# Two transformer blocks on one core: grouped products in the transitions, late weight splits, norm roots read from PSUM

## The chip, the cores and the metric

One core of a Trainium2 chip runs the whole program. The metric is device time in microseconds (us) from launch to end, lower is better. The engines are TensorE (PE in the profile, with its weight loads as PEld), VectorE (DVE), ScalarE (ACT), GpSimd (POOL) and SyncE (SP), which issues all DMAs here. Every engine has a queue of its own that runs in order; the engines meet only at semaphores.

## The reference, cut to what matters

The input is 512 tokens of width 1024, in float32. A first block (neighbourhood attention and gated linear attention, merge, SwiGLU feed-forward) is followed by two layers of a second block (latent attention, convolution and retention side by side, merge, feed-forward). What the change touches is the frame of these blocks:

```
h = rms_norm(x, ln_mix_pre[l])
proj = h @ w_in[l]                      # first products: wide()
...
x = x + rms_norm(merged @ w_out[l], ln_mix_post[l])
h = rms_norm(x, ln_ffn_pre[l])
f = (silu(h @ ffn_w_gate[l]) * (h @ ffn_w_up[l])) @ ffn_w_down[l]
x = x + rms_norm(f, ln_ffn_post[l])
```

with `rms_norm(x, g) = x * rsqrt(mean(x*x) + 1e-6) * g`. A place where one norm ends and the next products begin is called a transition below.

## The kernel before, in words

Activations lie transposed: 128 features on the partitions, 512 tokens in the free dimension, eight such pages for a width of 1024. Every float32 product is made of three fast ones. An input page x is split into a first part (`hi`, x rounded to fp32r) and a remainder (`lo` = x - hi), and so is every weight tile. A product step `mm` (L1628) issues three matmuls of 128x512 into one PSUM bank: whi with hi (L1640), whi with lo (L1641), wlo with hi (L1642). It waits first for both parts of the input.

Weights arrive as 429 blocks of eight tiles. `w_load` (a DMA by SP) brings a block into one of three raw buffers; `w_split` rounds it on ACT (L1972) into one of four whi buffers and subtracts on POOL (L2913) into wlo. Block b may be split only when block b-4 is used up (semaphore `wdone`). The splits are placed in the program by `w_ahead` as the tiles are named, one at every fourth tile at most.

A plan written out by hand (`planned`, class `Plan`) makes one list of steps; each engine walks through the list and runs the functions that bear a step's name. The order of the list is so the order of each engine's queue.

Four products with the same inputs are made together by `wide` (L211): for each of the eight input pages k, four `mm` steps, one for each of four weight columns in four banks. It is called six times: for the first four columns of the first block's `w_out`; for the start of the first block's feed-forward; and for the start of the mixer and of the feed-forward in each of the two layers. Its argument `feed` is a generator that makes the input pages (three steps ahead, then one for each k). In the layers it is `post_norm`, which on DVE adds the scaled page to x (L2845, L2849), and `Input.hi`, which makes `in_hi` on ACT (L2199), its square on ACT (L2202), the `in_lo` of the page before on DVE (L2640) and the running sum of squares on DVE (L2652). The mixer of the first layer is the exception: its pages are made during the feed-forward before it, and it has no feed. The inputs aren't divided by their root mean square ahead of the products, but the results are: so in the four wides of the layers the argument `late` holds two steps. `late[0]` (`Input.root`) sums the squares over partitions (`square_rows`, L1716, on PE) and takes the root (`root`: L2325 on DVE, L1994 on ACT, L2325 again). `late[1]` spreads the root over a PSUM bank (`spread`, L1729, PE: it waits for the last DVE step of the root, L2340). Before, `late[0]` stands after the last product of k = 6 and `late[1]` after the last of k = 7.

A norm after a product (`post_norm`, and `norm_x2` in the first block) has the same steps without products between them: `rstd_rows` issues `square_rows`, the `root`, one filler matmul (`keep_warm`, L1740, which appears as two instructions), the `spread`, and three fillers. In these four the squares come as two pages (a sum and a tail); in the late ones as one. `root` on DVE first copies the sums from the bank (L2330 and an addition L2332 for two pages, L2334 for one), ACT takes logarithm (L1998) and exponential (L2000), and three small DVE steps refine it by one Newton step (L2336, L2338, L2340).

Of the kernel before, what the change touches and what calls it, by code (L numbers as in the profile page):

```python
# [11 lines left out]
ALU = mybir.AluOpType  # L12
# [8 lines left out]
NR, NH = 3, 4  # L21
# [135 lines left out]
class Plan:  # L157
# [53 lines left out]
    def wide(self, items, xs, late=None, feed=(), homes=None):  # L211

        feed = iter(feed)
        for _ in range(3):
            next(feed, None)
        outs = [(homes[i] if homes else self.mb).take(("o", *item)) for i, item in enumerate(items)]
        for k in range(8):
            next(feed, None)
            for (name, m), o in zip(items, outs):
                s = self.w_next((name, m, k))  # L220
                self.step("mm", s, ((o, xs[k]),), k == 0, k == 7)
                if late is not None and k == 6 and o is outs[-1]:
                    late[0]()
                if late is not None and k == 7 and o is outs[-1]:
                    late[1]()
                yield

    def turned(self, items, xs, outs, k0=0, held=0, done=None):
# [62 lines left out]
class Squares:  # L291
# [40 lines left out]
    def rows(self, n, bks):  # L332

        p, t = self.p, self.tag
        bks.take(("qm", t))
        p.row_of[t] = len(p.row_of)
        p.step("square_rows", t, self.n, self.tail)
        for i in (0, self.tail):
            if i is not None:
                p.pages.give(("q", t, i), ("qm", t))  # L340
        p.step("root", t, n, self.tail is not None)

    def rstd_rows(self, n, bks):

# [1059 lines left out]
def program(nc, a, out, p):  # L1404
    with ExitStack() as ctx:
        def sb(name, shape, dt=F32):
            return ctx.enter_context(nc.sbuf_tensor(name, shape, dt))

        def sem(name):
            return ctx.enter_context(nc.semaphore(name))  # L1410
# [9 lines left out]
        whi = sb("whi", [128, NH, 8, 128], F32R)  # L1420
        wlo = sb("wlo", [128, NH, 8, 128], F32R)
# [17 lines left out]
        lin, dot, turn = (Signal(sem(n), at) for n in ("s_linear", "s_dot", "s_turn"))  # L1439
        whid, acp, fun = (Signal(sem(n), at) for n in ("s_whi", "s_copied", "s_function"))  # L1440
        vec = Signal(sem("s_vector"), at)
# [6 lines left out]
        def when(*name):  # L1448
            return at.get(name, (None, 0)) if counting[0] else at[name]
# [6 lines left out]
        ident, ones, bones = cst[:, 0, :], cst[:, 1, :], cst[:, 2, :]  # L1456
# [6 lines left out]
        def col(name, i=0, n=1):  # L1463
            o = PCOL[name][0] + i
            return prm[:, o:o + n]

        def F(name):
            return pageF[p.pages.place[name]][:, :]

        def R(name):  # L1470
            return pageR[p.pages.place[name]][:, :]

        def bank(name):
            return banks[p.mb.place[name] if name in p.mb.place else 4 + p.sbk.place[name]][:, :]
# [4 lines left out]
        def over(name):  # L1479

            for homes in (p.pages, p.mb, p.sbk):
                if name in homes.over:
                    return homes.over[name]

        def half(x, part):

            if x[0] == "HC":
                return R(x)[:, 0:256] if part == "hi" else R(x)[:, 256:512]
            return R((*x, part))
# [19 lines left out]
        def rows(t, i):  # L1509

            o = 256 + 12 * p.row_of[t] + 4 * i
            return smal[:, o:o + 4]
# [108 lines left out]
        def tensor(e):  # L1621
            w = Hand(e)

            def clear(name):
                for k in over(name):
                    w.wait_ge(*when(*k))

            def mm(s, groups, first, last):  # L1628
# [4 lines left out]
                for n, (name, x) in enumerate(groups):  # L1633
# [12 lines left out]
                    if names:  # L1646
                        i.then_inc(*lin.up(*names))

            def mm_turned(s, n, outs, x, first, last, final):
                a, ring = s % (8 * NH), 8 * NH  # L1650
                hi, lo = (y[:, :, :, :].rearrange("p b j f -> p (b j) f") for y in (whi, wlo))
                for b in range(s // 8, (s + n - 1) // 8 + 1):
                    w.wait_ge(*when("whi", b))
                    w.wait_ge(*when("wlo", b))
                w.wait_ge(*when(*x, "hi"))
                w.wait_ge(*when(*x, "lo"))
                for t, name in outs:
                    if first:
                        clear(name)
                    xh, xl = (half(x, part)[:, 128 * t:128 * t + 128] for part in ("hi", "lo"))  # L1660
                    for c, d in ((0, min(n, ring - a)), (ring - a, n)):
                        if c < d:
                            o, at0 = bank(name)[:, 128 * c:128 * d], (a + c) % ring
                            h, r = hi[:, at0:at0 + d - c, :], lo[:, at0:at0 + d - c, :]
                            e.matmul(o, xh, h, start=first and c == 0, stop=False, skip_group_check=True)  # L1665
                            e.matmul(o, xl, h, start=False, stop=False, skip_group_check=True)  # L1666
                            i = e.matmul(o, xh, r, start=False, stop=last and d == n, skip_group_check=True)  # L1667
                    names = [name] if last else []
                    if final and t == outs[-1][0]:
                        names += [("wdone", b) for b in range(s // 8, (s + n) // 8)]  # L1670
                    if names:
                        i.then_inc(*lin.up(*names))
# [43 lines left out]
            def square_rows(t, n, tail):  # L1716
                o = bank(("qm", t))
                clear(("qm", t))
                w.wait_ge(*when("cst"))
                w.wait_ge(*(when("q", t, 0) if n == 1 else when("qa", t, n - 1)))  # L1720
                for c, i in ((0, 0), (4, tail)):
                    if i is not None:
                        w.wait_ge(*when("q", t, i))
                        for j in range(4):
                            x = e.matmul(o[:, c + j:c + j + 1], F(("q", t, i))[:, 128 * j:128 * j + 128], ones[:, 0:1],
                                         start=True, stop=True)
                x.then_inc(*dot.up(("qm", t)))

            def spread(t):  # L1729
# [207 lines left out]
            def ret_values(l, h, i):  # L1937
# [6 lines left out]
                t.then_inc(*dot.up(("ro", l, h, i)))  # L1944

            mine = {f.__name__: f for f in (
                mm, mm_turned, mod_mm, first_sums, square_rows, spread, keep_warm, mod_columns, square_sum, to_tokens, x_turned, mod_sum,
                gla_gate, gla_gate_ctx, gla_state0, gla_states, gla_scores, gla_out, na_scores, na_values, mla_scores, mla_values, soft_rows, conv_mean, ret_scores,
                ret_values)}
            for kind, *what in p.steps:  # L1950
# [4 lines left out]
        def scalar(e):  # L1955
            w = Hand(e)
# [23 lines left out]
            def log_exp():  # L1980
                if loaded[0] != "both":
                    loaded[0] = "both"
                    e.preload_act_table_set("natural_log_exp_and_others")
# [7 lines left out]
                w.wait_ge(*fun.last())  # L1991
                e.activation(r, r, ACT.Exp, scale=-0.5).then_inc(*fun.up(("re", t)))

            def root(t, n, two):  # L1994
                x, r = rows(t, 2), rows(t, 0)
                log_exp()
                w.wait_ge(*when("qs", t))
                e.activation(r, x, ACT.Ln, scale=1.0 / n, bias=col("eps")).then_inc(*fun.up())  # L1998
                w.wait_ge(*fun.last())
                e.activation(r, r, ACT.Exp, scale=-0.5).then_inc(*fun.up(("re", t)))  # L2000
# [290 lines left out]
        def vector(e):  # L2291
            w = Hand(e)

            def clear(name):
                for k in over(name):
                    w.wait_ge(*when(*k))

            def after():
                w.wait_ge(*vec.last())
# [22 lines left out]
                after()  # L2322
                e.scalar_tensor_tensor(r, x, 1.5, r, ALU.add, ALU.mult).then_inc(*vec.up(("rr", t)))

            def root(t, n, two):  # L2325
                o = bank(("qm", t))
                r, s, x = (rows(t, i) for i in range(3))
                w.wait_ge(*when("qm", t))
                if two:
                    e.tensor_copy(s, o[:, 0:4]).then_inc(*vec.up())  # L2330
                    after()
                    e.tensor_tensor(x, s, o[:, 4:8], ALU.add).then_inc(*vec.up(("qs", t)))  # L2332
                else:
                    e.tensor_copy(x, o[:, 0:4]).then_inc(*vec.up(("qs", t)))  # L2334
                w.wait_ge(*when("re", t))
                e.scalar_tensor_tensor(s, r, -0.5 / n, r, ALU.mult, ALU.mult).then_inc(*vec.up())  # L2336
                after()
                e.scalar_tensor_tensor(s, x, n * EPS, s, ALU.add, ALU.mult).then_inc(*vec.up())  # L2338
                after()
                e.scalar_tensor_tensor(r, s, 1.5, r, ALU.add, ALU.mult).then_inc(*vec.up(("rcol", t)))  # L2340
# [600 lines left out]
        for engine in (sync, tensor, scalar, vector, gpsimd):  # L2941
            engine(Dry())
# [4 lines left out]
        block = ctx.enter_context(nc.Block())  # L2947
        block.sync(sync)
        block.tensor(tensor)
        block.scalar(scalar)  # L2950
        block.vector(vector)
# [181 lines left out]
```

## Time and profile before

| what | value |
|---|---|
| median of 3 runs | 2908.97 us (2908.12 to 2909.49) |
| profiled execution, its own time | 2907.14 us |
| its span, first to last instruction | 2905.3 us |
| PE busy | 2827.4 us, 97% |
| DVE, ACT, POOL busy | 1290.8, 1131.3, 1186.1 us |
| split on ACT, mean of 429 | 1053 ns |
| split on POOL, mean of 429 | 2427 ns |

A row of the timeline gives the start in the span, the duration, the engine, the line, what is written and read, how many like it were merged into the row, and in brackets how long the engine had been idle and who ended that. A matmul's duration contains its latency: in a dense stretch the starts are much closer than the durations.

### The profile page before, as it was taken

The page shows a single profiled execution, that of the slowest core. Times are in us where ns is not written, and L with a number is a line of the kernel's source. Part 1 is how long each engine was busy: PE and PEld are TensorE (multiplying, and loading weights), DVE is VectorE, ACT ScalarE, POOL GpSimd, SP SyncE. Part 2 cuts the span into 40 slices and gives each one's busy share as a digit, 9 for nine tenths or more (in the row PEclk, how much of TensorE's full clock was granted, in tenths as well). Part 3 has the DMA queues.
Part 4 walks back from the last instruction along what each step waited for, and adds up shares of the span by engine and source line. Part 5 has one row for each costly group of instructions (what it writes and reads, how often), then busy time and mean ns, then how long its engine had stood idle before and what let it go on. Part 6 is the DMA issues. An engine that isn't in the chain of part 4 may idle for free.

```text
span 2905.3 us, 34409 instructions
## 1 busy us (share of the span) xinstructions
PE 2827.4 (97%) x13708; PEld 2242.9 (77%) x13708; DVE 1290.8 (44%) x1714; ACT 1131.3 (39%) x1681; POOL 1186.1 (41%) x539
## 2 busy tenths in 40 slices
PE   7999999999999999999999999999999999999999
PEld 6787678788888776787787888867767868788887
DVE  4776424511113866835315202277677353341123
ACT  4334643432233555433334222245545233432222
POOL 2123233344443662453443444435624434344443
PEclk9999999999999999999999999999999999999999
DMA  7343223333333211232232323332102323233232
GB/s 255 116 152 126 76 83 99 110 113 96 96 100 125 80 59 37 72 94 73 88 123 77 98 94 102 95 104 79 66 30 73 102 66 110 93 98 99 94 95 80
DMA packets 89278, 277.97 MB, mean 96 GB/s; under 512 B 9952, under 2 KB 10272, under 8 KB 89120
## 3 DMA queue, kind: packets, MB, share of 16 engines
q1 hardware_dynamic: 89120, 275.78, 29.4%
q8 instruction: 109, 1.79, 0.3%
q14 instruction: 49, 0.40, 0.0%
HBM read 268.40 MB, written 7.34 MB: 95 GB/s over the span
## 4 chain that ended last, share of the span: by engine, by line
PE 87%; DVE 9%; ACT 3%; issue 1%; SPq 0%; DMA 0%; DVEq 0%; ACTq 0%
PE bank L1640 24%; PE bank L1642 24%; PE bank L1641 24%; PE bank L1750 2%; PE bank L1943 2%; PE bank L1893 2%; PE bank L1665 1%; PE bank L1666 1%; PE bank L1667 1%; PE bank L1905 1%; PE bank L1934 1%; DVE pageR L2640 1%; DVE pageF L2775 1%; PE bank L1710 1%; PE bank L1880 1%
## 5 line engine op out<-in xcount | busy, mean ns | idle before, releaser
L2913 POOL TENSOR_TENSOR wlo<-wraw,whi 128x1024 fp32r<-128x1024 f32 x429 | 1039.9, 2427 | 1489.5 <-ACT whi L1972 1482.1
L1640 PE MATMUL bank<-pageR,whi 128*128 128x512 f32 (+1 forms) x3376 | 1366.7, 405 | 20.0 <-DVE pageR L2640 8.2
L1642 PE MATMUL bank<-pageR,wlo 128*128 128x512 f32 (+1 forms) x3376 | 1306.4, 387 | 0.0
L1641 PE MATMUL bank<-pageR,whi 128*128 128x512 f32 (+1 forms) x3376 | 1305.5, 387 | 0.0
L1640 PEld LDWEIGHTS bank<-pageR,whi 128*128 128x128 f32 x3376 | 636.0, 188 | 186.7 <-issue 60.3
L1641 PEld LDWEIGHTS bank<-pageR,whi 128*128 128x128 f32 x3376 | 636.8, 189 | 143.6 <-issue 24.0
L1642 PEld LDWEIGHTS bank<-pageR,wlo 128*128 128x128 f32 x3376 | 635.4, 188 | 131.6
L1972 ACT ACTIVATE whi<-wraw 128x1024 fp32r<-128x1024 f32 x429 | 450.5, 1053 | 408.7 <-PE bank L1642 343.3
L2056 ACT ACTIVATE pageR<-pageF 128x512 fp32r<-128x512 f32 x136 | 86.0, 632 | 444.8 <-DVE pageF L2634 196.1
L2775 DVE SCALAR_TENSOR_TENSOR pageF<-pageF,prm 128x497 f32<-128x497 f32 (+9 forms) x180 | 200.0, 1111 | 2.7
L2629 DVE TENSOR_TENSOR pageF<-bank,pageF 128x512 f32<-128x512 f32 x44 | 30.4, 690 | 212.9 <-PE bank L1642 209.0
L2922 POOL TENSOR_TENSOR pageR<-pageF,pageR 128x512 fp32r<-128x512 f32 x46 | 66.0, 1450 | 137.3 <-ACT pageR L2056 129.7
L2086 ACT ACTIVATE pageF<-bank 128x512 f32<-128x512 f32 (+1 forms) x148 | 82.8, 575 | 96.4 <-PE bank L1750 95.9
L2157 ACT ACTIVATE pageF<-bank,smal 128x512 f32<-128x512 f32 x96 | 65.9, 686 | 135.2 <-DVE smal L2540 135.1
L2632 DVE TENSOR_TENSOR pageF<-pageF,bank 128x512 f32<-128x512 f32 x44 | 30.2, 687 | 197.0 <-PE bank L1642 163.7
L2933 POOL TENSOR_TENSOR pageF<-pageF 128x497 f32<-128x497 f32 (+14 forms) x60 | 82.2, 1370 | 67.9 <-ACT pageF L2252 67.3
L1750 PEld LDWEIGHTS bank<-cst,pageF 128*128 128x128 f32 x564 | 67.9, 141 | 45.2 <-ACT pageF L2157 15.8
L1750 PE MATMUL bank<-cst,pageF 128*128 128x128 f32 x564 | 85.0, 277 | 15.8 <-ACT pageF L2061 8.6
L2402 DVE TENSOR_TENSOR pageR<-pageF,pageR 128x512 fp32r<-128x512 f32 x90 | 67.1, 745 | 64.7 <-ACT pageR L2056 64.7
L2591 DVE SCALAR_TENSOR_TENSOR pageF<-pageF,bank 128x512 f32<-128x512 f32 x64 | 43.9, 685 | 110.2 <-PE bank L1642 109.9
L2226 ACT ACTIVATE pageF<-pageF 128x512 f32<-128x512 f32 x56 | 35.3, 631 | 140.6 <-DVE pageF L2695 140.6
L2312 DVE TENSOR_TENSOR pageF<-pageF 128x512 f32<-128x512 f32 x40 | 38.5, 963 | 115.3 <-ACT pageF L1978 114.9
(239 smaller groups left out, 2305.6 us busy)
## 6 DMA issues: line engine op xcount, KB each, us to landing
wraw<-in_wst SPq DMA_DIRECT2D x429, 512.0 KB, 3.5
pageF<-in_wmod SPq DMA_DIRECT2D x96, 256.0 KB, 4.5
pageF<-in_xT SPq DMA_DIRECT2D x16, 256.0 KB, 4.4
pageF<-in_bias SPq DMA_DIRECT2D x16, 256.0 KB, 3.9
kept<-pageF SPq DMA_DIRECT2D x16, 256.0 KB, 4.5
pageF<-kept SPq DMA_DIRECT2D x16, 256.0 KB, 4.0
out_x<-pageF SPq DMA_DIRECT2D x8, 256.0 KB, 2.0
pageF<-in_cT SPq DMA_DIRECT2D x4, 256.0 KB, 6.4
```

Source lines behind the costliest of these rows:

```text
L1640: e.matmul(o, hi, xh, start=first, stop=False)
L1641: e.matmul(o, hi, xl, start=False, stop=False)
L1642: i = e.matmul(o, lo, xh, start=False, stop=last)
L1750: t = e.transpose(o[:, 128 * j:128 * j + 128], x[:, c:c + 128], ident)
L1972: e.activation(whi[:, b % NH, :, :], wraw[:, b % NR, :, :], ACT.Copy).then_inc(*whid.up(("whi", b)))
L2056: e.activation(R((*x, "hi")), F(src), ACT.Copy).then_inc(*acp.up((*x, "hi")))
L2086: e.activation(F(dst)[:, 0:n], bank(("tb", dst))[:, 0:n], ACT.Copy).then_inc(*acp.up(dst))
L2402: e.tensor_tensor(R((*x, "lo")), F(src), bc(R((*x, "hi"))), ALU.subtract).then_inc(*vec.up((*x, "lo")))
L2775: e.scalar_tensor_tensor(acc, x, c, acc, ALU.mult, ALU.add).then_inc(*vec.up(("tapd", l, m, n)))
L2913: e.tensor_tensor(wlo[:, b % NH, :, :], wraw[:, b % NR, :, :], bc(whi[:, b % NH, :, :]), ALU.subtract).then_inc(*wlod.up(("wlo", b)))
L2922: e.tensor_tensor(R((*x, "lo")), F(src), bc(R((*x, "hi"))), ALU.subtract).then_inc(*low.up((*x, "lo")))
L2933: e.tensor_tensor(acc, acc, F(("tap", l, n))[:, 0:hi - lo], ALU.add).then_inc(*low.up(("tapd", l, m, n)))
```

## The change

In `wide`, the four products of one k are no longer four `mm` steps but two: `mm_first_part` waits for the `hi` of the page and issues whi·hi and wlo·hi for all four columns, `mm_second_part` waits for the `lo` and issues whi·lo for all four. `late[0]` now stands between the two parts of k = 7, `late[1]` behind the second. The splits that `w_ahead` would place at k = 1 to 4 are left to k = 5, 6 and 7. In `square_rows` both pages of squares are summed in the bank, and `root` reads this bank itself, on ACT and in the middle DVE step; the copy and the addition on DVE are gone.

```diff
         for k in range(8):
             next(feed, None)
-            for (name, m), o in zip(items, outs):
-                s = self.w_next((name, m, k))
-                self.step("mm", s, ((o, xs[k]),), k == 0, k == 7)
-                if late is not None and k == 6 and o is outs[-1]:
-                    late[0]()
-                if late is not None and k == 7 and o is outs[-1]:
-                    late[1]()
+            slots = [self.w_slot((name, m, k)) for name, m in items]
+            if k == 0 or k > 4:
+                self.w_ahead(*slots)
+            self.step("mm_first_part", tuple(slots), tuple(outs), xs[k], k == 0)
+            if late is not None and k == 7:
+                late[0]()
+            self.step("mm_second_part", tuple(slots), tuple(outs), xs[k], k == 7)
+            if late is not None and k == 7:
+                late[1]()
+            for _ in items:
                 yield
...
+            def mm_first_part(slots, outs, x, first):
+                xh = half(x, "hi")
+                w.wait_ge(*when(*x, "hi"))
+                for s, name in zip(slots, outs):
...
+                    e.matmul(bank(name), whi[:, b % NH, j, :], xh, start=first, stop=False)
+                    e.matmul(bank(name), wlo[:, b % NH, j, :], xh, start=False, stop=False)
+
+            def mm_second_part(slots, outs, x, last):
+                xl = half(x, "lo")
+                w.wait_ge(*when(*x, "lo"))
+                for s, name in zip(slots, outs):
...
+                    i = e.matmul(bank(name), whi[:, b % NH, j, :], xl, start=False, stop=last)
...
+                pages_in = (0,) if tail is None else (0, tail)
+                for i in pages_in:
+                    w.wait_ge(*when("q", t, i))
+                    for j in range(4):
+                        x = e.matmul(o[:, j:j + 1], F(("q", t, i))[:, 128 * j:128 * j + 128], ones[:, 0:1],
+                                     start=i == 0 and j == 0, stop=i == pages_in[-1] and j == 3, skip_group_check=True)
...
             # root on ACT
-                x, r = rows(t, 2), rows(t, 0)
+                x, r = bank(("qm", t))[:, 0:4], rows(t, 0)
-                w.wait_ge(*when("qs", t))
+                w.wait_ge(*when("qm", t))
...
             # root on DVE
-                o = bank(("qm", t))
-                r, s, x = (rows(t, i) for i in range(3))
+                x, r, s = bank(("qm", t))[:, 0:4], rows(t, 0), rows(t, 1)
                 w.wait_ge(*when("qm", t))
-                if two:
-                    e.tensor_copy(s, o[:, 0:4]).then_inc(*vec.up())
-                    after()
-                    e.tensor_tensor(x, s, o[:, 4:8], ALU.add).then_inc(*vec.up(("qs", t)))
-                else:
-                    e.tensor_copy(x, o[:, 0:4]).then_inc(*vec.up(("qs", t)))
```

## Rows read from the trace of the kernel before

**Rows 1.** The page's busy times: engine, us, share, instructions.
```profile
PE 2827.4 (97%) x13708; PEld 2242.9 (77%) x13708; DVE 1290.8 (44%) x1714; ACT 1131.3 (39%) x1681; POOL 1186.1 (41%) x539
```

**Rows 2.** Timeline, root of the norm ahead of layer 0's feed-forward.
```profile
1523.17 0.16 DVE L2330 COPY smal<-bank 128x4 f32<-128x4 f32 x1 [5.86 <-PE bank L1725]
...
1523.56 0.30 ACT L1998 ACTIVATE smal<-smal,prm 128x4 f32<-128x4 f32 x1 [1.04 <-DVE smal L2332]
...
1524.74 0.38 PE L1733 MATMUL bank<-cst,smal 128*128 128x128 f32 x1 [0.63 <-DVE smal L2340]
```

**Rows 3.** Timeline, layer 0's feed-forward wide: the feed and PE's waits.
```profile
1529.71 0.47 PE L1640 MATMUL bank<-pageR,whi 128*128 128x512 f32 x1 [1.24 <-ACT pageR L2199]
...
1535.99 2.50 POOL L2913 TENSOR_TENSOR wlo<-wraw,whi 128x1024 fp32r<-128x1024 f32 x1 [15.41 <-ACT whi L1972]
...
1536.16 2.88 DVE L2640 SCALAR_TENSOR_TENSOR pageR<-pageF,prm,pageR 128x512 fp32r<-128x512 f32 x1
...
1539.19 0.47 PE L1640 MATMUL bank<-pageR,whi 128*128 128x512 f32 x1 [1.07 <-DVE pageR L2640]
...
1546.60 0.47 PE L1640 MATMUL bank<-pageR,whi 128*128 128x512 f32 x1 [1.69 <-DVE pageR L2640]
```

**Rows 4.** Line L2640, all 32 of it: ns min/median/max.
```profile
L2640 DVE SCALAR_TENSOR_TENSOR pageR<-pageF,prm,pageR x32: 739/744/2885, 861.9 to 2549.4; 128x512 fp32r<-128x512 f32 x32
```

**Rows 5.** Timeline, the end of the same wide.
```profile
1548.47 0.73 ACT L2199 ACTIVATE pageR<-pageF,prm 128x512 fp32r<-128x512 f32 x1 [3.53 <-DVE pageF L2849]
...
1549.62 1.99 ACT L1972 ACTIVATE whi<-wraw 128x1024 fp32r<-128x1024 f32 x2
...
1550.83 4.74 POOL L2913 TENSOR_TENSOR wlo<-wraw,whi 128x1024 fp32r<-128x1024 f32 x2 [4.93 <-ACT whi L1972]
...
1552.16 0.95 PE L1725 MATMUL bank<-cst,pageF 128*128 128x1 f32 x8
...
1553.90 1.69 DVE L2336 SCALAR_TENSOR_TENSOR smal<-smal 128x4 f32<-128x4 f32 x1 [0.60 <-ACT smal L2000]
...
1556.04 1.16 PE L1733 MATMUL bank<-cst,smal 128*128 128x128 f32 x8
```

**Rows 6.** Timeline near 952 us: DVE and POOL, instructions behind each other.
```profile
951.73 1.37 DVE L2772 TENSOR_SCALAR pageF<-pageF,prm 128x512 f32<-128x512 f32 x1
...
952.78 5.36 POOL L2913 TENSOR_TENSOR wlo<-wraw,whi 128x1024 fp32r<-128x1024 f32 x2
...
953.14 2.75 DVE L2775 SCALAR_TENSOR_TENSOR pageF<-pageF,prm 128x497 f32<-128x497 f32 x1
```

**Rows 7.** Line L2629, which reads one bank and one page: ns min/median/max.
```profile
L2629 DVE TENSOR_TENSOR pageF<-bank,pageF x44: 681/691/693, 1557.9 to 2832.9; 128x512 f32<-128x512 f32 x44
```

**Rows 8.** Timeline, the end of layer 0's mixer wide.
```profile
925.94 0.16 DVE L2334 COPY smal<-bank 128x4 f32<-128x4 f32 x1 [16.56 <-PE bank L1725]
...
928.62 1.05 PE L1733 MATMUL bank<-cst,smal 128*128 128x128 f32 x8
```

**Rows 9.** Windows: busy us (count) of each engine, granted clock (PEclk), DMA share, GB/s.
```profile
83.42:90.23 6.81, 5.98 (x20) 5.27 (x21) 5.70 (x11) 3.71 (x10) 0.00 (x0) 0.50 0.00 0
540.80:544.20 3.40, 3.40 (x11) 1.97 (x10) 0.68 (x5) 0.50 (x2) 0.00 (x0) 0.50 0.00 0
1230.30:1233.70 3.40, 1.27 (x6) 0.62 (x4) 3.00 (x5) 3.32 (x4) 1.20 (x1) 1.00 0.00 0
1233.70:1237.10 3.40, 3.40 (x9) 2.31 (x8) 1.16 (x2) 2.53 (x3) 1.44 (x1) 0.50 0.25 31
```

**Rows 10.** Timeline, matmuls at the lower granted clock.
```profile
1235.56 0.63 PE L1640 MATMUL bank<-pageR,whi 128*128 128x512 f32 x1
1235.99 0.63 PE L1641 MATMUL bank<-pageR,whi 128*128 128x512 f32 x1
```

**Rows 11.** Timeline, PE's waits in layer 1's mixer and feed-forward wide.
```profile
1939.66 0.67 PE L1710 MATMUL bank<-pageF,cst 128*128 128x512 f32 x1 [0.93 <-DVE pageF L2312]
...
2546.37 0.47 PE L1640 MATMUL bank<-pageR,whi 128*128 128x512 f32 x1 [1.68 <-DVE pageR L2640]
```

More of the change, by code:

```diff
@@ L340, in rows @@
                 p.pages.give(("q", t, i), ("qm", t))
-        p.step("root", t, n, self.tail is not None)
+        p.step("root", t, n)
     def rstd_rows(self, n, bks):
@@ L1647, in mm @@
                         i.then_inc(*lin.up(*names))
+            def mm_first_part(slots, outs, x, first):
+                xh = half(x, "hi")
+                w.wait_ge(*when(*x, "hi"))
+                for s, name in zip(slots, outs):
+                    b, j = divmod(s, 8)
+                    w.wait_ge(*when("whi", b))
+                    w.wait_ge(*when("wlo", b))
+                    if first:
+                        clear(name)
+                    e.matmul(bank(name), whi[:, b % NH, j, :], xh, start=first, stop=False)
[4 more added lines that the diff above has]
+                for s, name in zip(slots, outs):
+                    b, j = divmod(s, 8)
+                    i = e.matmul(bank(name), whi[:, b % NH, j, :], xl, start=False, stop=last)
+                    names = [name] if last else []
+                    if j == 7:
+                        names.append(("wdone", b))
+                    if names:
+                        i.then_inc(*lin.up(*names))
             def mm_turned(s, n, outs, x, first, last, final):
@@ L1720, in square_rows @@
                 w.wait_ge(*(when("q", t, 0) if n == 1 else when("qa", t, n - 1)))
[L1721 to L1726, printed above, removed]
+                pages_in = (0,) if tail is None else (0, tail)
[4 more added lines that the diff above has]
+                                     start=i == 0 and j == 0, stop=i == pages_in[-1] and j == 3, skip_group_check=True)
                 x.then_inc(*dot.up(("qm", t)))
@@ L1946, in tensor @@
             mine = {f.__name__: f for f in (
-                mm, mm_turned, mod_mm, first_sums, square_rows, spread, keep_warm, mod_columns, square_sum, to_tokens, x_turned, mod_sum,
+                mm, mm_first_part, mm_second_part, mm_turned, mod_mm, first_sums, square_rows, spread, keep_warm, mod_columns, square_sum, to_tokens, x_turned, mod_sum,
                 gla_gate, gla_gate_ctx, gla_state0, gla_states, gla_scores, gla_out, na_scores, na_values, mla_scores, mla_values, soft_rows, conv_mean, ret_scores,
@@ L1992, in rstd_act, with root @@
                 e.activation(r, r, ACT.Exp, scale=-0.5).then_inc(*fun.up(("re", t)))
-            def root(t, n, two):
-                x, r = rows(t, 2), rows(t, 0)
+            def root(t, n):
+                x, r = bank(("qm", t))[:, 0:4], rows(t, 0)
                 log_exp()
-                w.wait_ge(*when("qs", t))
+                w.wait_ge(*when("qm", t))
                 e.activation(r, x, ACT.Ln, scale=1.0 / n, bias=col("eps")).then_inc(*fun.up())
@@ L2323, in rstd_dve, with root @@
                 e.scalar_tensor_tensor(r, x, 1.5, r, ALU.add, ALU.mult).then_inc(*vec.up(("rr", t)))
-            def root(t, n, two):
-                o = bank(("qm", t))
-                r, s, x = (rows(t, i) for i in range(3))
+            def root(t, n):
+                x, r, s = bank(("qm", t))[:, 0:4], rows(t, 0), rows(t, 1)
                 w.wait_ge(*when("qm", t))
-                if two:
-                    e.tensor_copy(s, o[:, 0:4]).then_inc(*vec.up())
-                    after()
-                    e.tensor_tensor(x, s, o[:, 4:8], ALU.add).then_inc(*vec.up(("qs", t)))
-                else:
-                    e.tensor_copy(x, o[:, 0:4]).then_inc(*vec.up(("qs", t)))
                 w.wait_ge(*when("re", t))
```

## The prediction

> **What bounds the kernel now.** I read the busy times first. PE is busy 97% of the span [rows 1], so time can only be won where PE waits, or lost where it comes to wait. Next I went through PE's rows in order of time for the brackets that show a wait, and looked up the regions that the change touches, with all engines side by side. Seven places matter: four norms after a product, in which nothing but fillers covers the root; three wides with a feed (layer 0's feed-forward, both of layer 1's); and the late steps of all four layer wides (the fourth is layer 0's mixer, whose pages are ready).
>
> In a norm, from the copy of the sums to the spread are 1.57 us, and PE idles 0.63 us before the spread [rows 2].
>
> In a wide with a feed PE waits three times, 1.24, 1.07 and 1.69 us [rows 3]; the other two have the same waits, the last of them 1.68 us in layer 1's feed-forward [rows 11]. The first is the first page's remainder. The others have a cause that lies on POOL. At 1535.99 the split's subtraction starts; at 1536.16 DVE starts `in_lo`, and it takes 2.88 us instead of the line's median of 0.74 [rows 3, 4]. It ends 0.5 us after POOL's. So DVE stood still while POOL subtracted. A step that reads a bank and a page shows nothing of the kind in 44 cases, 681 to 693 ns [rows 7]. The root has it too: its first DVE step, of four columns, takes 1.69 us from 1553.90, and ends where POOL's second subtraction ends, 1550.83 + 4.74 = 1555.57 [rows 5]. When POOL has one subtraction behind another, a blocked DVE step gets in between: the one started at 951.73 ends at 953.10, next to POOL's start at 952.78, and the next one, from 953.14, is held again to 955.89 [rows 6]. This is the point on which my forecast rests.
>
> **The root read from the bank.** Two DVE steps go where there are two pages: 1523.56 - 1523.17 = 0.39 us; for one page I take half, 0.20 [rows 2]. The middle DVE step now reads a bank and one small page, so POOL can't hold it [rows 7]; the first and the third still read two operands in SBUF. That the read from a bank costs ACT or DVE more is not seen: L2629 with a bank is at 0.69 us [rows 7]; bounds -0.1 to +0.1 us a step, I take 0. In the norm ahead of the first feed-forward the 0.39 us are PE's own waiting. The clock is at 1.2 GHz there (0.50 granted from 540.80 to 544.20 [rows 9]) and fillers follow that run slower if they come earlier, so I count -0.3 (0 to -0.39). The other three norms stand in front of wides, below. The number of matmuls is unchanged, so summing in the bank costs nothing.
>
> **First parts ahead, in layer 0's feed-forward.** The start: PE needs only the first page's `hi`, so the 1.24 us go and PE starts about 1.6 us earlier with the norm's 0.39. Of this little is left at k = 3: the split of k = 0 stays where it was, behind the fourth `in_hi` on ACT, and still holds `in_lo` of that page. This one is released at 1539.19 - 0.39 = 1538.80. What moves is that only four matmuls of k = 3 wait for it instead of twelve. The split of k = 2, which made the 1.69 us, goes behind the feed, and DVE's feed is 2.88 - 0.74 = 2.14 us earlier from there on: 2.53 with the norm. A matmul takes (1552.16 - 1546.60)/24 = 0.23 us [rows 3, 5]. The feed makes a page in less than twelve of them, so nothing more waits, and from 1538.80 PE has 4 + 36 + 8 = 48 matmuls to `square_rows`: 1538.80 + 11.04 = 1549.84, where before it was 1552.16. So 2.3 us are won up to this point.
>
> **The end of that wide.** In the old order twelve products (2.8 us) covered the root, now it is four (0.9 us). From `square_rows` to the root's first DVE step it was 1553.90 - 1552.16 = 1.74 us, less the copy 1.54: 1551.38. PE ends its second part at 1549.84 + 0.95 + 0.92 = 1551.7.
> But the deferred splits are now all here. ACT has three, not two, right behind the last `in_hi` and square: from 1549.62 - 2.53 = 1547.1, done by 1550.1, so ACT's part of the root isn't late. POOL's three start at 1550.83 - 2.53 = 1548.30 and take 4.74/2 = 2.37 us each [rows 5]: they end at 1550.67, 1553.04 and 1555.41. The root's first DVE step (1551.38) meets the second subtraction and gets in at 1553.04. The middle one is free. The third comes 0.2 us later, meets the third subtraction, and ends with it at 1555.4. The spread follows at 1555.5, against 1556.04 before. Of the 2.3 us just 0.54 are left, and PE idles 3.8 us in one piece where it idled 4 us in three. The spread releases all that follows, so this is the gain of the whole wide. The splits themselves come no later: the last one ends at 1555.4 where the last ended at 1555.57, and the loads behind them on SP's queue wait for nothing new. If this cover were gone, each us of delay would be one of the span, as PE is dense behind.
>
> **The other wides.** Layer 1's two have the same waits and the same order: -0.54 each. In layer 0's mixer wide nothing waits for pages. There the order costs: ACT's part of the root starts eight matmuls after the old copy, 925.94 + 1.84 = 927.78, the spread comes 1.57 - 0.39 = 1.18 us later, at 928.96, against 928.62 [rows 8]: +0.34. ACT is idle there, so the splits go as soon as blocks are free and don't move. The first block's two wides have no wait and no late step: 0.
>
> **The clock.** An idle piece of 3.8 us is new in this part of the kernel. At 1233.06 a wait of PE ended, in a stretch with 1.27 us busy of 3.40; the granted clock then was 0.50 for 3.4 us [rows 9]: 2.4 GHz became 1.2. A matmul takes 0.43 us in it [rows 10]. In the old feed-forward wides no stretch at 0.50 shows. I expect one in each of the three: behind the idle piece it costs 3.4 x (1 - 0.23/0.43) = 1.6 us if all of it falls on dense work, nothing if it falls into the wait. I take 1.1, nearer to what happened at 1233.7. In layer 1's mixer PE waits 0.93 us for DVE soon after [rows 11] and that swallows most: 0.2.
> The Trainium skill, TensorE: Matmul & The Clock Gate, "What's actually happening", says that the throttled clock is the default state and that activity releases it. By it the sum below keeps its 2.4 us for the clock; were only the average share of work to count, those would be dropped and the kernel would come out 1.6 us faster.
>
> **The sum.** -0.3 (norm) + 0.34 (layer 0's mixer) - 3 x 0.54 (wides) + 1.1 + 1.1 + 0.2 (clock) = +0.8 us. The profiled execution took 2907.14 us (2905.3 and 1.8 around it) and lies 1.8 us under the median; the difference carries over: 2908.97 + 0.8 = 2909.8 us.
>
> **Rivals.**
> *One subtraction is escaped* (0.14). If `square_rows` came 0.7 us earlier, the root's first step would meet the first subtraction (to 1550.67) and the third step the second, to 1553.04. Spread at 1553.1, 2.9 us gained in each, no long idle: -8.7, so 2900.3 us. For: the margin is only 0.7 us in a chain of 11 us. Against: both ends hang on the same DVE feed.
> *The root runs free* (0.12). If the small steps slip in, or the split of k = 0 no longer meets `in_lo` (it started just 0.17 us ahead, 1535.99 against 1536.16 [rows 3]), the spread comes 1.54 + 0.61 us after `square_rows`, about 1552.0: -4.05 each, -12.2 in all, 2896.8 us. Against: the 1.69 us of [rows 5].
> *The clock stays low* (0.09), the case on the slow side. From 83.42 to 90.23 it was 0.50 for 6.8 us [rows 9]. If the fall comes inside the idle piece at the spread and a second such stretch joins on, about 5 to 6.8 us of dense work run at 0.43 us: 2.4 to 3.2 us each, less 0.9 in layer 1's mixer. +6.3 to +8.7 - 1.6: 2914 to 2916 us. [...] Against: in [rows 9] one wait of some 2 us brought one short stretch.
> *The change doesn't do what it says* (0.03): another wait holds k = 3 or the first part, and all stays within 1 us.
>
> **How the numbers follow.** The forecast has 0.62. What this kernel's measurement can tell from no change is 0.2%, 5.8 us: below 2903.2 or above 2914.8. Faster are the first two rivals and little else: 0.27. Slower is most of the third, 0.09. The rest, 0.64, is the same. The range takes in the first rival and most of the third and leaves out the second: 2899 to 2915 us. The forecast's own range is 2907 to 2913.
>
> **What would show it.** Three POOL subtractions back to back just after the last `in_hi` of a wide; L2336 and L2340 both long there (up to 2.4 us) and L2338 short; PE waiting some 3.8 us before the spread for L2340; one `in_lo` at 2.9 us in each wide, not two; no wait at k = 0 and about 0.7 us ahead of the second part of k = 3; 0.3 us ahead of the spread in layer 0's mixer; a granted clock of 0.50 after three of the spreads. If L2340 stays at 0.16 us everywhere, the forecast is wrong and a rival holds.

## The result, and the profile after

| | before | changed |
|---|---|---|
| median of 17 runs | 2910.32 us | 2914.87 us |
| profiled execution's span | 2905.3 us | 2912.3 us |
| PE busy | 2827.4 us | 2834.4 us |

The ratio is 1.0018 (1.0011 to 1.0024): the change costs 0.18%, some 5 us. It was forecast at +0.8 us. The spans of the two profiled executions differ by 7.0 us, the medians by 4.55: the profiled executions took 2907.14 and 2914.15 us, so they lie 3.2 and 0.7 us under their medians. PE did the same 13708 matmuls and was busy 7 us longer, which no wait explains; this points to the clock.

In the lines of the changed kernel the first DVE step of the root is L2356, the middle one L2358, the last L2360; the spread is L1760, `square_rows` L1752, the second part L1669, `in_lo` L2660, the split L1999 on ACT and L2933 on POOL. The norm ahead of layer 0's feed-forward, timeline of the changed kernel (it answers to [rows 2]):

```profile
1524.38 0.26 ACT L2025 ACTIVATE smal<-bank,prm 128x4 f32<-128x4 f32 x1 [0.65 <-PE bank L1752]
...
1524.98 0.16 DVE L2356 SCALAR_TENSOR_TENSOR smal<-smal 128x4 f32<-128x4 f32 x1 [6.46 <-ACT smal L2027]
1525.18 0.16 DVE L2358 SCALAR_TENSOR_TENSOR smal<-bank,smal 128x4 f32<-128x4 f32 x1
1525.37 0.16 DVE L2360 SCALAR_TENSOR_TENSOR smal<-smal 128x4 f32<-128x4 f32 x1
1525.59 0.60 PE L1760 MATMUL bank<-cst,smal 128*128 128x128 f32 x3 [0.28 <-DVE smal L2360]
```

ACT starts where the copy was, and reads the bank in 0.26 us instead of 0.30; the middle DVE step is 0.16 us as before. PE's wait is 0.28 us instead of 0.63. Then the wide behind it, first the middle (it answers to [rows 3]):

```profile
1536.85 2.50 POOL L2933 TENSOR_TENSOR wlo<-wraw,whi 128x1024 fp32r<-128x1024 f32 x1 [15.06 <-ACT whi L1999]
1537.01 2.89 DVE L2660 SCALAR_TENSOR_TENSOR pageR<-pageF,prm,pageR 128x512 fp32r<-128x512 f32 x1
...
1539.96 0.51 PE L1669 MATMUL bank<-pageR,whi 128*128 128x512 f32 x1 [0.47 <-DVE pageR L2660]
```

and its end (it answers to [rows 5]):

```profile
1548.36 2.94 ACT L1999 ACTIVATE whi<-wraw 128x1024 fp32r<-128x1024 f32 x3
...
1549.57 7.01 POOL L2933 TENSOR_TENSOR wlo<-wraw,whi 128x1024 fp32r<-128x1024 f32 x3 [10.22 <-ACT whi L1999]
...
1551.01 0.95 PE L1752 MATMUL bank<-cst,pageF 128*128 128x1 f32 x8
1551.82 1.19 PE L1669 MATMUL bank<-pageR,whi 128*128 128x512 f32 x4
...
1552.61 1.69 DVE L2356 SCALAR_TENSOR_TENSOR smal<-smal 128x4 f32<-128x4 f32 x1 [2.92 <-ACT smal L2027]
1554.33 0.16 DVE L2358 SCALAR_TENSOR_TENSOR smal<-bank,smal 128x4 f32<-128x4 f32 x1
1554.53 2.07 DVE L2360 SCALAR_TENSOR_TENSOR smal<-smal 128x4 f32<-128x4 f32 x1
```

All three subtractions are back to back. The root's first step is held to the end of the second. The middle one reads a bank and passes during the third. The last one is held to the end of the third. The spreads of the three wides with a feed, PE's timeline:

```profile
1556.65 1.65 PE L1760 MATMUL bank<-cst,smal 128*128 128x128 f32 x6 [3.64 <-DVE smal L2360]
...
1933.75 1.65 PE L1760 MATMUL bank<-cst,smal 128*128 128x128 f32 x6 [3.67 <-DVE smal L2360]
...
2560.02 1.22 PE L1760 MATMUL bank<-cst,smal 128*128 128x128 f32 x4 [3.66 <-DVE smal L2360]
```

and layer 0's mixer (it answers to [rows 8]):

```profile
929.64 1.16 PE L1760 MATMUL bank<-cst,smal 128*128 128x128 f32 x8 [0.21 <-DVE smal L2360]
```

What comes behind the long waits, windows of the changed kernel (it answers to [rows 9]; the granted clock is the number after POOL's):

```profile
1555.70:1562.50 6.80, 5.85 (x18) 4.99 (x19) 2.72 (x4) 2.51 (x3) 0.88 (x1) 0.50 0.37 142
1562.50:1570.00 7.50, 7.50 (x35) 6.18 (x34) 4.21 (x7) 4.32 (x6) 1.36 (x1) 1.00 0.00 0
1931.10:1937.90 6.80, 4.15 (x14) 3.67 (x15) 3.87 (x6) 2.04 (x4) 2.90 (x3) 0.50 0.74 246
2559.20:2566.00 6.80, 5.98 (x18) 5.11 (x19) 2.72 (x4) 2.51 (x3) 0.75 (x1) 0.50 0.37 146
```

The clock is at 1.2 GHz for 6.8 us, not 3.4. It falls inside the wait, 2.7 us after its start in layer 0's feed-forward (at 1555.7, where the spread starts at 1556.65), 1.0 us in the mixer (at 1931.1) and 2.8 us in layer 1's feed-forward (at 2559.2). Behind it, matmuls start 0.43 us apart:

```profile
1558.95 0.63 PE L1644 MATMUL bank<-pageR,whi 128*128 128x512 f32 x1
1559.38 0.63 PE L1645 MATMUL bank<-pageR,wlo 128*128 128x512 f32 x1
```

To place the time I take the distances between spreads, from the timelines of each kernel (us). The other kernels are described with the experiments below. Up to the norm where the first column starts, changed, old_late, both and ffn_behind are 0.3 to 0.9 us later than before and fill is 1.8; two_splits is 6.5 us later, 4.2 of them lost behind the spread of layer 0's mixer against the changed kernel.

| kernel | norm to spread, layer 0's feed-forward | to the next norm | norm to spread, layer 1's mixer | to the next norm | norm to spread, layer 1's feed-forward | to the end |
|---|---|---|---|---|---|---|
| before | 31.30 | 342.62 | 31.19 | 594.66 | 31.31 | 349.48 |
| changed | 31.06 | 345.38 | 31.72 | 595.22 | 31.05 | 352.28 |
| fill | 31.07 | 343.16 | 31.73 | 594.27 | 31.07 | 349.46 |
| two_splits | 27.63 | 342.27 | 27.50 | 598.53 | 27.63 | 349.50 |
| old_late | 29.68 | 342.30 | 29.59 | 595.96 | 28.78 | 349.54 |
| ffn_behind | 27.61 | 342.29 | 30.98 | 595.95 | 27.63 | 349.47 |
| both | 28.54 | 342.29 | 28.67 | 594.35 | 27.62 | 349.51 |

The two feed-forward wides won what was forecast, nearly nothing. The loss lies behind them: 2.76 and 2.80 us behind the feed-forward spreads, 0.6 us behind the mixer's (0.95 against fill). Some norms have a low stretch of the clock of their own, which makes a number 0.5 to 0.9 us larger: changed and fill in the second and third column, old_late in the first and third, both in the first. In old_late and ffn_behind a low stretch near 2232 us makes the fourth number 1.6 us larger. With such a stretch layer 1's mixer wide is 0.53 us longer in the changed kernel, and not shorter. The price of the first long wait is thus known less well than the 2.80 us of the last. Against fill the second column is 2.2 us longer, but fill's own stretch at that norm is 6.8 us and the changed kernel's is 3.4, so this is too little; against the kernels without a stretch there (342.3) it is 3.1 us, which is too much. The profile before has no low stretch at that norm; why the changed kernel and fill have one isn't known.

### The profile page after: what moved, and what is told of

Its sections match the earlier page's. It is cut to its first block, busy times and chain, and to the rows that moved or that the text cites. A ratio compares the mean times of both kernels' runs of the same rounds, so it can differ in the third digit from the quotient of the medians.

```text
span 2912.3 us, 34371 instructions
## 1 busy us (share of the span) xinstructions
PE 2834.4 (97%) x13708; PEld 2250.6 (77%) x13708; DVE 1294.3 (44%) x1702; ACT 1131.1 (39%) x1681; POOL 1184.6 (41%) x539
## 4 chain that ended last, share of the span: by engine, by line
PE 87%; DVE 9%; ACT 2%; issue 1%; SPq 0%; DMA 0%; DVEq 0%; ACTq 0%
PE bank L1643 23%; PE bank L1645 23%; PE bank L1644 23%; PE bank L1970 2%; PE bank L1777 2%; PE bank L1920 2%; PE bank L1692 1%; PE bank L1693 1%; PE bank L1694 1%; PE bank L1662 1%; PE bank L1661 1%; PE bank L1669 1%; PE bank L1932 1%; PE bank L1961 1%; DVE pageF L2595 1%
## 5 line engine op out<-in xcount | busy, mean ns | idle before, releaser
L2933 POOL TENSOR_TENSOR wlo<-wraw,whi 128x1024 fp32r<-128x1024 f32 x429 | 1038.5, 2423 | 1498.0 <-ACT whi L1999 1497.4
L1643 PE MATMUL bank<-pageR,whi 128*128 128x512 f32 x3184 | 1293.4, 406 | 8.1 <-DVE pageR L2398 3.2
L1645 PE MATMUL bank<-pageR,wlo 128*128 128x512 f32 x3184 | 1234.6, 388 | 0.0
L1644 PE MATMUL bank<-pageR,whi 128*128 128x512 f32 x3184 | 1233.3, 387 | 0.0
L1643 PEld LDWEIGHTS bank<-pageR,whi 128*128 128x128 f32 x3184 | 601.6, 189 | 162.1 <-issue 43.0
L1644 PEld LDWEIGHTS bank<-pageR,whi 128*128 128x128 f32 x3184 | 601.8, 189 | 136.5 <-issue 23.9
L1645 PEld LDWEIGHTS bank<-pageR,wlo 128*128 128x128 f32 x3184 | 600.3, 189 | 123.8
L1999 ACT ACTIVATE whi<-wraw 128x1024 fp32r<-128x1024 f32 x429 | 450.3, 1053 | 407.1 <-PE bank L1645 318.9
```

Source lines behind the costliest of these rows:

```text
L1643: e.matmul(o, hi, xh, start=first, stop=False)
L1644: e.matmul(o, hi, xl, start=False, stop=False)
L1645: i = e.matmul(o, lo, xh, start=False, stop=last)
L1999: e.activation(whi[:, b % NH, :, :], wraw[:, b % NR, :, :], ACT.Copy).then_inc(*whid.up(("whi", b)))
L2933: e.tensor_tensor(wlo[:, b % NH, :, :], wraw[:, b % NR, :, :], bc(whi[:, b % NH, :, :]), ALU.subtract).then_inc(*wlod.up(("wlo", b)))
```

## The experiments

My theory after the result: (1) POOL's subtractions set the time of the spread; (2) the long wait that they leave in one piece brings the clock down for 6.8 us, and this is the loss. The rival: the new order of the products, or its extra waits, costs by itself. All these kernels were timed beside the kernel before.

**fill.** The wait is filled.

```diff
+                fill()          # p.keep_warm(sbk, 3) in the three wides with a feed
                 late[1]()
```

> The changed kernel with three filler matmuls (six instructions, some 2.8 us) between the second part of k = 7 and the spread, in the three wides with a feed. Theory (trap and clock): POOL's three subtractions still hold the spread at the same time, but PE no longer idles 3.6 us, so no stretch at 0.50 follows the spread and the 2.8 us per feed-forward wide go: ratio to before 0.9995 (0.998 to 1.000). Rival (the new order of products and waits itself costs, the low clock is a bystander): ratio stays at 1.0018.

Measured: 0.9999 (0.9990 to 1.0008). PE waits 1.08 us instead of 3.64, the spread comes at the same distance (31.07 against 31.06 us), and the clock holds, in the windows around the spread:

```profile
1550.00:1557.00 7.00, 6.52 (x28) 4.20 (x26) 4.04 (x5) 2.72 (x5) 6.47 (x3) 1.00 0.34 87
1557.00:1564.00 7.00, 6.39 (x32) 5.47 (x33) 3.14 (x5) 3.15 (x4) 0.53 (x1) 1.00 0.39 140
```

So the loss is the clock's: work that computes nothing wins it back. The rival falls: fill has the new order and all other waits, and costs nothing against before.

**last_split** and **two_splits.** Splits go behind the spread.

```diff
-            if k == 0 or k > 4:
-                self.w_ahead(*slots)
+            if k == 0 or k > 4:
+                if late is not None and k in (6, 7):      # last_split: (7,)
+                    held.extend(slots)
+                else:
+                    self.w_ahead(*slots)
...
                 late[1]()
+                for s in held:
+                    self.w_ahead(s)
```

> The changed kernel, but where a wide has late steps only the split of k = 7 is placed behind the spread. Theory (trap): the first DVE step of the root is held by the second subtraction (about 1.7 us), the third step is free, the spread is 2.9 us earlier than before the change, PE idles 1.3 us, no low clock: ratio 0.997. Rival (the number of subtractions doesn't matter, only ACT's queue does): spread earlier by ACT's 1 us only, low clock stays, ratio 1.001.

Measured: 0.9989 (0.9980 to 0.9997). The mechanism is as expected, DVE's timeline of last_split:

```profile
1553.70 1.69 DVE L2361 SCALAR_TENSOR_TENSOR smal<-smal 128x4 f32<-128x4 f32 x1 [2.90 <-ACT smal L2032]
1555.43 0.16 DVE L2363 SCALAR_TENSOR_TENSOR smal<-bank,smal 128x4 f32<-128x4 f32 x1
1555.62 0.16 DVE L2365 SCALAR_TENSOR_TENSOR smal<-smal 128x4 f32<-128x4 f32 x1
```

One step is held instead of two. The size is a third of what I expected. A part goes in the mixers, where the deferred split holds another chain (below), and a part to the clock: PE waits 1.74 us, and behind that there still is a low stretch, here of 3.4 us:

```profile
1556.30:1559.70 3.40, 3.40 (x13) 2.92 (x12) 0.69 (x1) 2.11 (x3) 0.42 (x1) 0.50 0.56 161
```

> The changed kernel, but where a wide has late steps the splits of k = 6 and 7 are placed behind the spread; that of k = 5 stays. Theory (trap): the root's first DVE step comes 0.7 us after the only subtraction ahead of it, both long steps go back to 0.16 us, the spread comes about 4 us earlier than before the change in each of three wides, PE idles 0.3 us ahead of it, no low clock: ratio 0.9958 (0.995 to 0.997). Rival (splits placed late starve the weights, or the root is held by something else than POOL): PE waits for wlo behind the spread, ratio 1.000 or more.

Measured: 0.9981 (0.9973 to 0.9990). No root step is held, and norm to spread is 27.50 to 27.63 us: 3.7 less than before, 4.0 with the norm's 0.35, in all three wides. But less than half of these 12 us arrives. The rest, some 8 us, is lost in the mixers, where the deferred subtractions meet other DVE steps. POOL's and DVE's timelines of two_splits, layer 0's mixer, and PE's:

```profile
934.04 7.97 POOL L2938 TENSOR_TENSOR wlo<-wraw,whi 128x1024 fp32r<-128x1024 f32 x3 [16.65 <-ACT whi L2004]
```
```profile
937.00 2.77 DVE L2730 TENSOR_TENSOR pageF<-pageF 32x512 f32<-32x512 f32 x1
939.80 2.76 DVE L2732 TENSOR_TENSOR pageF<-pageF 32x512 f32<-32x512 f32 x1
```
```profile
945.09 1.10 PE L1742 MATMUL bank<-pageF,cst 128*128 128x512 f32 x2 [3.52 <-DVE pageF L2344]
```

PE waits 3.52 us there where it waited 0.92 in the changed kernel, and the stretch behind layer 1's mixer is 598.53 us instead of the 594.66 of before (here a low stretch of 3.4 us, behind another wait of 3.50 us, takes a part). In this kernel a subtraction has its price where DVE has a chain that PE waits for; behind a feed-forward spread it shows none (342.27 us to the next norm, as in old_late and both).

**early_splits.** The splits are where they were, products and root as changed.

```diff
-            if k == 0 or k > 4:
-                self.w_ahead(*slots)
+            self.w_ahead(*slots)
```

> The changed kernel with the splits at k = 2, 4 and 6 again, as before the change. Theory: the split of k = 2 holds one in_lo for 2.9 us again, the first parts hide part of it, square_rows comes 0.5 us earlier than before the change, one root step is held by the second of two subtractions, the spread is 0.4 us earlier than before and PE idles 2.0 us ahead of it, which may or may not bring a low stretch: ratio 0.9995 to 1.0005. Rival (grouping the products alone costs): ratio 1.0015 or more with the same clock as before.

Measured: 1.0001 (0.9992 to 1.0010). PE waits 1.65 us for a held `in_lo` again and 1.87 us ahead of the spread. Two of the three spreads are followed by a low stretch of 3.4 us. Grouping the products, with the new root, shows neither a cost nor a gain in the time as long as the splits aren't late; what the grouping alone would be worth without these low stretches no run shows.

**splits_only.** The kernel before with the late splits alone.

```diff
                 s = self.w_slot((name, m, k))        # was w_next
+                if k == 0 or k > 4:
+                    self.w_ahead(s)
```

> The kernel before with only the splits of k = 1 to 4 left to k = 5, 6 and 7. Theory: the wait of 1.69 us at k = 5 goes; square_rows comes 1.9 us earlier; the root, still with its copy, meets the second subtraction with its first step and the third with its second (its middle step reads SBUF here): spread at about the old time, PE idles some 2.2 us ahead of it, perhaps with a low stretch: ratio 1.0000 to 1.0010. Rival (late splits alone are the gain and the grouping is the loss): ratio 0.998 or less.

Measured: 1.0002 (0.9993 to 1.0011). Here the middle step of the root has both operands in SBUF, and it is the one that the third subtraction holds:

```profile
1554.81 1.54 DVE L2338 SCALAR_TENSOR_TENSOR smal<-smal 128x4 f32<-128x4 f32 x1 [0.60 <-ACT smal L2002]
1556.38 2.27 DVE L2340 SCALAR_TENSOR_TENSOR smal<-smal 128x4 f32<-128x4 f32 x1
1558.69 0.16 DVE L2342 SCALAR_TENSOR_TENSOR smal<-smal 128x4 f32<-128x4 f32 x1
```

Norm to spread is 31.30 us, as before to the hundredth: what the late splits win at the feed, the root gives back. The first and second step are held and the third is free, as forecast.

**root_only.** The root read from the bank, all else as before.

> The kernel before with the root read from the bank alone: products in single steps, splits and late steps in the old places. Theory: four norms are 0.39 us shorter, the root's middle step can't be held; the spreads come 0.4 us earlier: -1.5 us, ratio 0.9995 (0.999 to 1.000). Rival (reading the bank costs ACT or DVE some 0.1 to 0.2 us a step and the norms gain nothing): ratio 1.000 and the span from copy to spread unchanged at 1.57 us.

Measured: 1.0000 (0.9991 to 1.0008). The norm is shorter as expected, PE waits 0.28 us instead of 0.63 ahead of the spread. In the profiled execution layer 1's mixer spread comes 0.8 us earlier than before; a low stretch of the clock at 2233.8, which the profile of before hasn't, then takes this back. This measurement can't tell a gain of 1.5 us from none: the rows show shorter norms, the times show no gain.

**old_late.** The root goes back behind k = 6.

```diff
-            if late is not None and k == 7:
-                late[0]()
             self.step("mm_second_part", tuple(slots), tuple(outs), xs[k], k == 7)
+            if late is not None and k == 6:
+                late[0]()
```

> The changed kernel with late[0] (square_rows and root) back behind k = 6, splits late as changed. Theory: square_rows comes 1.3 us earlier than in the changed kernel, the root's first step meets the first subtraction and its third the second, and ACT does the third split only after the root: the spread is some 2.9 us earlier than before the change in three wides, twelve products stand ahead of it so PE idles about 1.4 us, no long low clock; in layer 0's mixer nothing is lost. Ratio 0.997. Rival (the place of the root is without effect, only the number of splits ahead counts as program order has it): the third step is held by the third subtraction all the same, ratio 1.000 or more.

Measured: 0.9973 (0.9964 to 0.9982), as forecast. DVE's and PE's timelines of old_late:

```profile
1552.05 0.50 DVE L2356 SCALAR_TENSOR_TENSOR smal<-smal 128x4 f32<-128x4 f32 x1 [1.77 <-ACT smal L2027]
1552.58 0.16 DVE L2358 SCALAR_TENSOR_TENSOR smal<-bank,smal 128x4 f32<-128x4 f32 x1
1552.78 2.10 DVE L2360 SCALAR_TENSOR_TENSOR smal<-smal 128x4 f32<-128x4 f32 x1
```
```profile
1554.93 1.16 PE L1760 MATMUL bank<-cst,smal 128*128 128x128 f32 x8 [0.68 <-DVE smal L2360]
```

Its first step comes 0.5 us ahead of the end of the first subtraction, in the changed kernel 0.7 us behind it. It is the same chain of steps and the same subtractions; which of them it meets differs, and that is 2.3 us in a wide (28.78 against 31.05). PE's wait is 0.7 us instead of 3.6. No low stretch follows the spreads of these wides.

**ffn_behind.** The two splits go behind the spread in the layers' feed-forward wides only (`behind=rs is not None`); layer 1's mixer has fillers.

> The changed kernel with the splits of k = 6 and 7 behind the spread in the two feed-forward wides of the layers only, three filler matmuls ahead of the spread in layer 1's mixer, and layer 0's mixer as changed. Theory: each feed-forward wide keeps its 4 us, and the 3.9 us that two_splits lost in each mixer (two DVE steps of the rope behind the spread held by subtractions, 2.8 us each) don't come back: some -8.7 us against before, ratio 0.997. Rival (what two_splits lost belongs to the low stretches of the clock, wherever they fall): ratio 0.998 to 0.999 again.

Measured: 0.9977 (0.9968 to 0.9986), between the two forecasts, so the ratio doesn't decide. The table does: each feed-forward wide keeps its 3.7 us, no wait of 3.5 us shows in the mixers, and the stretch behind layer 1's mixer is 2.6 us shorter than in two_splits although both kernels have one low stretch of 3.4 us in it. So at least this part of what two_splits lost belongs to the subtractions. The span is 2899.0 us, 6.3 below before's.

**both.** `late[0]` as in old_late in the mixers, splits as in ffn_behind in the feed-forwards.

> The two better forms put together: in the feed-forward wides of the layers the splits of k = 6 and 7 behind the spread and late[0] between the parts of k = 7; in the two mixer wides late[0] behind k = 6 and the splits late as changed. Theory (each wide's price is its own): two feed-forward wides give 4.1 us each, layer 1's mixer 1.6 to 2.5 us, the norm 0.3, layer 0's mixer nothing: -11 us, ratio 0.9962 (0.995 to 0.997). Rival (what is won at a spread is lost again behind it): 0.9973 as old_late.

Measured: 0.9963 (0.9949 to 0.9977), median 2898.13 us beside 2908.51 for before: the lowest median, 0.37% under the kernel before and some 0.55% under the changed one. Its interval overlaps with that of old_late, so it isn't shown to be faster than that one. In the two feed-forward wides the root runs free, and the clock is at 2.4 GHz behind the spread (in layer 1's mixer the root's last step is still held, 2.11 us):

```profile
1553.05 0.16 DVE L2363 SCALAR_TENSOR_TENSOR smal<-smal 128x4 f32<-128x4 f32 x1 [2.89 <-ACT smal L2034]
...
1553.44 0.16 DVE L2367 SCALAR_TENSOR_TENSOR smal<-smal 128x4 f32<-128x4 f32 x1
```
```profile
1553.66:1560.40 6.74, 6.74 (x34) 5.72 (x35) 1.73 (x3) 4.41 (x5) 3.83 (x2) 1.00 0.27 84
```

## Why the prediction was right and wrong

The waits came out as worked out, in number, place and size. The term that failed is the clock's, and it was the largest.

- *The norms*: PE's wait shrank by 0.35 us (0.39 forecast) ahead of layer 0's feed-forward. In the norm ahead of the first feed-forward, `square_rows` to spread went from 2.66 to 2.31 us (0.3 forecast; 2.51 in root_only). Reading the bank costs nothing more.
- *The feed*: one `in_lo` held, none at k = 0 waited for. PE waited 0.47 us at k = 3 (0.7 forecast).
- *The trap*: both long steps are there, 1.69 and 2.07 us, the middle one 0.16; PE's wait is 3.64 to 3.67 us (3.8 forecast). The spreads of the two feed-forwards came 0.24 to 0.26 us nearer to their norms, 0.6 with the norm's part (0.54 forecast); that of layer 1's mixer is 0.53 us farther, with a low stretch of the clock at its norm that the forecast hadn't. That a bank operand frees the middle step rested on [rows 7], which doesn't say whether POOL was at work: the trace of before has 33 of these 44 steps overlapping a subtraction, so the reading holds.
- *Layer 0's mixer*: 0.21 us of wait (0.3 forecast). But the time from the norm ahead of the first feed-forward to this spread grew from 386.38 to 387.02 us, by 0.64 (+0.34 forecast). With the root back behind k = 6 (old_late) it still is 386.71: the place of the root is about half of it, and what the other half is stays open.
- *The clock*: this is the step that failed. "I expect one in each of the three: behind the idle piece it costs 3.4 x (1 - 0.23/0.43) = 1.6 us if all of it falls on dense work, nothing if it falls into the wait. I take 1.1." The low stretch was 6.8 us and not 3.4, and some 5.9 us of it lay on work in each feed-forward: 2.2 to 3.1 us in layer 0's and 2.8 us in layer 1's, against 1.1. In the mixer PE's wait for DVE vanished in it, as forecast, and it still cost 0.6 to 0.95 us against 0.2. With 2.6 (an estimate, the middle of 2.2 and 3.1), 2.8 and 0.8 for the clock the sum is -0.3 + 0.3 - 1.8 + 2.6 + 2.8 + 0.8 = +4.4 us; the medians differ by 4.55. So close an agreement is partly luck: the sum holds neither the low stretch at layer 1's mixer norm nor the 0.3 us more of layer 0's mixer.

The longer stretch was in [rows 9], at 83.42, and it stood among the rivals (*the clock stays low*) with 0.09 and 2914 to 2916 us. Its mechanism is what came. That 2914.87 lies in its bounds is luck in part: the kernel before was at 2910.32 us in this measurement and not at 2908.97, and as a difference the rival had +4.7 to +7.1 us where +4.55 was measured. I had put more weight on the stretch behind a wait of 2.1 us than on this one, and the prediction doesn't name the wait ahead of this one. It is in the timeline of the kernel before:

```profile
84.25 1.54 PE L1750 MATMUL bank<-cst,pageF 128*128 128x128 f32 x6 [4.88 <-ACT pageF L2061]
```

A wait of 4.88 us, with the fall 0.8 us ahead of its end. The wait that I forecast, 3.8 us, lies between 2.1 and 4.9, and the fall inside the wait is what the changed kernel shows too. The sentence of the Trainium skill (TensorE: Matmul & The Clock Gate, "What's actually happening"), that activity releases the throttle, agrees with the trace: during the wait the level fell, and it rose 4.2 to 6.0 us after work was back. On the two fast rivals: the subtraction that was to be escaped was missed by 0.7 us, as worked out, and old_late shows what it is worth.

What stays open: what sets the length of a low stretch. After waits of 3.64 to 3.67 us it was 6.8 us three times; after waits of 1.7 to 2.0 us (last_split, early_splits, splits_only) it was 3.4 us at five of nine spreads and none at four; after 0.65 to 1.1 us (old_late, fill, ffn_behind) there was none. In the three long ones the fall came 2.7, 1.0 and 2.8 us after the start of the wait, and the stretch was as long each time.

## What to carry to other kernels

When waits are moved, look where they collect: three waits of 4.0 us in all cost 4 us, one wait of 3.6 us cost some 6, since the clock fell during it. Where one engine can hold another, a job that is put off from one chain lands on the next; place it where PE waits for no chain of the held engine, and work out which of the instructions meets which, as 0.7 us decided over 2.3. And when a forecast rests on one of two rows of the same kind, look up what came before each of them.

## What the runs showed of the hardware that I had not expected

- A DVE step of four columns (0.16 us when free) is held to the end of a subtraction as one of 512 is: it took 2.07 us in the changed kernel and 2.27 in splits_only. With one operand in a bank it took 0.16 us in the midst of a subtraction.
- Three filler matmuls in a wait of 3.65 us kept the clock at 2.4 GHz and were worth 2.2 us or more and 2.8 us behind the two feed-forward spreads, without moving them.
- ACT's step on four columns took 0.26 us from a bank, against 0.30 from SBUF.
